# Turning a sample's cached keys on VectorE instead of TensorE, through a DRAM scratch, in a decoder step

## The chip, the cores and the metric

One core of one Trainium2 chip runs the kernel. The metric is the device time of one execution in microseconds (us), as the median of several runs. All arithmetic is float32.

## What is computed

One inference step of a two-layer decoder for a prompt of 256 tokens and a sample group of 8 sequences with one new token each, which share the weights. The first layer mixes by convolution and gating and ends in a dense feed-forward part; the second attends and ends in a mixture of experts. The part that the change touches is the sample's attention over its 1024 cached keys, which lie in pages:

```python
def dsa_attend(q, qi, wi, qpos, kidx, gather_kv, topk):
    dots = jnp.einsum('bthd,bsd->bths', qi, kidx) * (IDX_DIM ** -0.5)
    score = jnp.einsum('bth,bths->bts', wi, jax.nn.relu(dots))
    score = jnp.where(admissible, score, -jnp.inf)
    top_val, sel = lax.top_k(score, topk)
    k_sel, v_sel = gather_kv(sel)
    logits = jnp.einsum('btkgd,btskd->btkgs', qg, k_sel) * (HEAD_DIM ** -0.5)
    p = jax.nn.softmax(jnp.where(valid, logits, -jnp.inf), axis=-1)
    return jnp.einsum('btkgs,btskd->btkgd', p, v_sel)
```

For the prompt the same function runs over its own 256 keys (64 are chosen); for the sample 256 of 1025 are chosen, by page table from cache_k and cache_v. There are 16 query heads, 4 key heads and 64 dimensions a head.

## The kernel before

The five engines run hand-ordered programs that meet in semaphores. The stages, by the semaphore numbers of the finished TensorE groups (eight matmuls of a 128-row output each): input and output projection of the even layer, **up** (G_UP, 44 groups; `hidden` on VectorE multiplies two groups per step m), **down**, the odd layer's input projection (G_OIN, 18 groups, with rotation, index scores and top-k beside it), **attention**, output projection, routing, experts.

In the attention stage the prompt is worked in eight units u = 0 to 7, each one block of 128 queries and four heads; units 0 to 3 see 128 keys, units 4 to 7 see 256. Each unit has two halves. Its steps are: `logits(u)` on TensorE into two PSUM banks; `masked_logits(u)` on VectorE (mask, then row maximum, one of each per half); `exps(u, half)` on ScalarE; `probs_t(u, half)`, transposes on TensorE into bank 6; `probs_by_key(u, half)`, the copy of that bank on ScalarE; `values(u, half)` on TensorE; `heads(u)` on VectorE; `heads_t(u)` on TensorE and `heads_out(u)` on ScalarE. There is one bank 6, so the second half's `probs_t` waits for the copy of the first half. Two buffers S hold the exponentials of neighbouring units.

Between these steps stands the sample's work. The cached keys come from DRAM by indirect DMAs on GpSimd's queue (`gather_k`, 16 of them, 512 KB each), key by row. `k_unit` transposes four 128x128 blocks on TensorE, and `k_copy` on ScalarE moves the result into KT: 32 units of each. `k_logits` multiplies four sequences' keys with the queries, 512 columns each, into banks 2 and 3. The sample's choice of 256 keys is a radix search on VectorE: `radix(s)` counts over 1032 scores, `tally(s)` on TensorE sums the counts, `refine(s)` narrows the threshold; after eight rounds come ties (`eqk`, a scan), the masked logits SS, their maximum, the exponential on ScalarE, transposes, and `sample_values(par)`, 32 matmuls each. `select` finds the prompt's top 64 by rounds of max and match-replace. At the end VectorE writes the sample's heads into yT and raises `so_done`; the output projection on TensorE and the first loads of expert weights on SyncE's queue wait for it.

The input projection's rotation has its cosine part on GpSimd (`cosine`), queued behind `gather_k` of the first four; VectorE's `turn` waits for it.

## Time and profile before

| | us |
|---|---|
| median of 3 runs | 873.46 (873.28 to 873.88) |
| span of the profiled execution, first to last instruction | 871.0 |
| device time around the span, at the median of the runs | 2.5 |
| TensorE busy | 832.9 (96%) |
| VectorE busy | 246.1 (28%) |
| ScalarE busy | 139.4 (16%) |
| GpSimd busy | 98.7 (11%) |
| DMA: moved, mean rate | 206.02 MB, 237 GB/s |

The profiled execution's own device time is not recorded beside its span; 873.46 is taken for it. Busy shares are averages over stages that have different limits. A TensorE line counts matmuls whose ends are modelled, so a busy TensorE need not work at its peak. "PEclk" is the granted TensorE clock as a share of 2.4 GHz: 1.00 is that level and 0.50 is 1.2 GHz. A float32 matmul of the program shows as two records in the trace, a transpose as one.

### The profile page before, as it was taken

What the parts mean: (1) busy time and instruction counts of PE and PEld (TensorE: products, weight loads), DVE (VectorE), ACT (ScalarE), POOL (GpSimd) and SP (SyncE); (2) the same over time, 40 slices, a digit from 0 to 9 for tenths busy, and PEclk for the clock granted to TensorE, in tenths of its full rate; (3) what the DMA queues carried; (4) which work ended last, traced back from release to release, by engine and by line L of the source; (5) the groups of instructions that cost most, each with busy time, mean ns of one, the idle gap of its engine ahead of it and who ended that gap; (6) DMA issues with size and microseconds to landing.
All of it is one profiled execution on the core that took longest, in us unless ns stands there. A gap on an engine that the chain in (4) does not pass through costs nothing.

```text
span 871.0 us, 13710 instructions
## 1 busy us (share of the span) xinstructions
PE 832.9 (96%) x5826; PEld 565.2 (65%) x5826; DVE 246.1 (28%) x706; ACT 139.4 (16%) x342; POOL 98.7 (11%) x146
## 2 busy tenths in 40 slices
PE   6999999999999999999998989999999899999996
PEld 5888878888888888877676566864543343343332
DVE  2173216000000000074566861154422011021025
ACT  0020113000000011131225762121000010000010
POOL 4300300000000000021221410003200001010120
PEclk9999999999999999999997988999999999999998
DMA  9799733448240048897023480977999999999961
GB/s 295 269 376 365 251 97 96 155 136 259 67 133 1 1 136 261 206 218 184 3 96 121 154 334 5 394 278 283 369 410 395 410 392 411 394 394 411 400 254 50
DMA packets 106491, 206.02 MB, mean 237 GB/s; under 512 B 23558, under 2 KB 60818, under 8 KB 105412
## 3 DMA queue, kind: packets, MB, share of 16 engines
q1 hardware_dynamic: 93540, 166.68, 54.5%
q0 software_dynamic: 9264, 31.95, 10.6%
q10 hardware_dynamic: 3632, 6.59, 2.2%
q8 instruction: 43, 0.70, 0.3%
q14 instruction: 12, 0.10, 0.0%
HBM read 192.51 MB, written 12.69 MB: 236 GB/s over the span
## 4 chain that ended last, share of the span: by engine, by line
PE 76%; SPq 9%; DVE 6%; DMA 5%; issue 2%; ACT 2%; DVEq 0%; ACTq 0%
PE ps L685 45%; PE ps L1252 9%; SPq L360 8%; PE ps L1280 3%; DMA scr<-moe_w 2%; DMA slot<-moe_w 2%; PE ps L736 2%; PE ps L1319 2%; PE ps L1072 1%; PE ps L1189 1%; PE ps L1015 1%; PE ps L1088 1%; PE ps L1023 1%; PE ps L898 1%; PE ps L1055 1%
## 5 line engine op out<-in xcount | busy, mean ns | idle before, releaser
L685 PE MATMUL ps<-rw,slot 128*128 128x264 f32 x640 | 142.6, 385 | 0.0
L685 PEld LDWEIGHTS ps<-rw,slot 128*128 128x128 f32 x640 | 120.8, 189 | 21.6
L1252 PE MATMUL ps<-slot,hT 128*32 128x512 f32 x1104 | 123.2, 599 | 3.2 <-DMA slot<-moe_w 3.1
L685 PE MATMUL ps<-xw,slot 128*128 128x264 f32 x512 | 120.6, 392 | 0.8 <-issue 0.8
L685 PEld LDWEIGHTS ps<-xw,slot 128*128 128x128 f32 x512 | 97.0, 192 | 19.4 <-issue 2.3
L1252 PEld LDWEIGHTS ps<-slot,hT 128*32 128x32 f32 x1104 | 40.8, 111 | 80.6 <-issue 69.4
L685 PE MATMUL ps<-hT,slot 128*128 128x264 f32 x352 | 79.8, 386 | 0.0
L685 PEld LDWEIGHTS ps<-hT,slot 128*128 128x128 f32 x352 | 66.3, 190 | 10.9
L1280 PE MATMUL ps<-slot,hT 128*32 128x256 f32 x1216 | 68.1, 380 | 0.0
L685 PE MATMUL ps<-yT,slot 128*128 128x264 f32 x256 | 59.4, 388 | 0.5 <-DVE yT L2082 0.5
L1280 PEld LDWEIGHTS ps<-slot,hT 128*32 128x32 f32 x1216 | 38.2, 110 | 25.7 <-issue 1.0
L685 PEld LDWEIGHTS ps<-yT,slot 128*128 128x128 f32 x256 | 47.8, 190 | 10.2 <-DVE rw L1683 0.8
L1858 DVE TENSOR_TENSOR hT<-silu,ps 128x264 f32<-128x264 f32 x20 | 8.6, 429 | 130.9 <-PE ps L685 130.9
L1623 ACT ACTIVATE silu<-ps 128x256 f32<-128x256 f32 x22 | 8.4, 383 | 210.4 <-PE ps L1252 207.6
L2241 DVE TENSOR_TENSOR yT<-silu,ps 128x256 f32<-128x256 f32 x19 | 8.0, 421 | 110.6 <-ACT silu L1623 110.6
L555 POOL DMA_INDIRECT rw<-cache_k,idx x4 | 3.8, 949 | 293.9 <-PE ps L736 280.1
L1252 PE MATMUL ps<-scr,hT 128*32 128x512 f32 x304 | 34.0, 593 | 0.8 <-DMA scr<-moe_w 0.7
L1434 ACT ACTIVATE silu<-ps 128x264 f32<-128x264 f32 x20 | 7.8, 390 | 128.6 <-PE ps L685 128.6
L1683 DVE SCALAR_TENSOR_TENSOR xw<-rw,ps 128x264 f32<-128x264 f32 x8 | 3.4, 429 | 80.6 <-PE ps L685 80.6
L1252 PEld LDWEIGHTS ps<-scr,hT 128*32 128x32 f32 x304 | 10.1, 110 | 23.3 <-issue 20.2
L639 POOL DMA_DIRECT2D r_rows<-yT x28 | 15.2, 547 | 69.2 <-DVE yT L2246 68.7
L2246 DVE COPY yT<-ps 128x256 f32<-128x256 f32 x19 | 8.1, 425 | 50.3 <-PE ps L1280 50.3
(467 smaller groups left out, 858.3 us busy)
## 6 DMA issues: line engine op xcount, KB each, us to landing
slot<-moe_w SPq DMA_DIRECT2D x50, 1024.0 KB, 19.3
slot<-moe_w SPq DMA_DIRECT2D x16, 2048.0 KB, 15.7
slot<-ffn_w SPq DMA_DIRECT2D x22, 1024.0 KB, 8.0
scr<-moe_w SPq DMA_DIRECT2D x14, 1024.0 KB
slot<-ffn_w SPq DMA_DIRECT2D x8, 1408.0 KB, 6.6
slot<-w_in_even SPq DMA_DIRECT2D x4, 2048.0 KB, 20.5
r_rows<-silu ACTq DMA_DIRECT2D x1, 6144.0 KB, 31.5
slot<-w_out_even SPq DMA_DIRECT2D x2, 2048.0 KB, 24.7
```

Source lines behind the costliest of these rows:

```text
L360: sp.dma_start(dst, src).then_inc(slab_in[s], 16)
L639: pool.dma_start(rows[:, :, 256 * j:256 * j + 256], orow[32 * j:32 * j + 32, 0:nt]).then_inc(rows_stored, 16)
L685: mm = pe.matmul(out, lhs(k), rhs(k), start=(k == 0), stop=(k == n - 1))
L736: mm = pe.matmul(out, lhs(k), scaled[:, k, :], start=(k == 0), stop=(k == KD - 1))
L898: pe.matmul(ps[4][:, 0:T], rot, hT[:, n, :], start=True, stop=True).then_inc(rot_done, 1)
L1015: mm = pe.transpose(ps[i % 2][:, P * r:P * r + P], kraw[n % 2][j][:, 256 * r + P * jj:256 * r + P * jj + P], ident)
L1023: mm = pe.matmul(ps[2 + hf][32 * j:32 * j + 32, :], qw[:, jj, 2 * j + par, 16 - 16 * par:48 - 16 * par], KT[par][:, j, jj, :], start=(par ...
L1055: mm = pe.transpose(ps[6][:, P * (c * nb + k):P * (c * nb + k) + P], S[u % 2][:, half, c, P * k:P * k + P], ident)
L1072: mm = pe.matmul(ps[7][:, P * c + 64 * half:P * c + 64 * half + 64], PT[v % 2][:, P * (c * nb + k):P * (c * nb + k) + P], ktv[:, k, 256 + ...
L1252: mm = pe.matmul(ps[t][32 * j:32 * j + 32, :].rearrange("p (w n) -> p w n", w=2), xgT[:, cap * k + 32 * t:cap * k + 32 * t + 32], moe_slab ...
L1280: mm = pe.matmul(ps[4 + t][32 * j:32 * j + 32, 0:256], hTs[:, t, m % 2, 32 * (m // 2):32 * (m // 2) + 32], moe_slab(4 + m // 4, i)[:, m % ...
L1319: return pe.matmul(ps[4 + half][0:CAP, :], hTl[:, m % 2, m // 2, :], moe_slab(4 + m // 4, i)[:, m % 4, 512 * half:512 * half + 512], start ...
```

## The change

The sample's keys are no longer turned in the attention stage. During the up projection GpSimd gathers each sequence's 1 MB of keys into SBUF (into xw or sqT), VectorE transposes it in 32x32 blocks with one instruction per sequence (`turn_keys`, after every second `hidden` from m = 4 on), and GpSimd stores it with four DMAs into a scratch in DRAM, `k_turned`, in the order the matmuls need. Later eight loads of 1 MB on SyncE's queue bring it back into eight areas. `k_unit`, `k_copy` and the 16 gathers beside the attention are gone; the values are gathered into the same areas once the key products are done. The order of the attention stage on TensorE, ScalarE and VectorE is written anew. The core of the diff:

```diff
...
+        kraw = [flat2(a)[:, 0:2048] for a in (xw, sqT)]
+        kturn = [flat2(yT)[:, 0:2048], cache[:, 0:2048]]
+        area = [[flat2(rw)[:, 0:2048], flat2(sqT)[:, 0:2048], slot[0][:, 0:2048], slot[0][:, 2048:4096]],
+                [slot[2][:, 0:2048], slot[2][:, 2048:4096], slot[3][:, 0:2048], slot[3][:, 2048:4096]]]
...
+            sp.wait_ge(k_turn_stored[1], 256)
...
+            def load_keys(par, j):
+                sp.dma_start(area[par][j], k_turned[2 * j + par]).then_inc(k_in[par], 16)
+            sp.wait_ge(group_done, G_OIN + 4)
+            load_keys(0, 0)
+            load_keys(0, 1)
...
+            sp.wait_ge(sdots_done, 1)
+            load_keys(0, 2)
+            load_keys(0, 3)
+            sp.wait_ge(group_done, G_OIN + 14)
+            load_keys(1, 0)
+            load_keys(1, 1)
+            sp.wait_ge(group_done, G_OIN + 18)
+            load_keys(1, 2)
+            load_keys(1, 3)
...
+            off = lambda b: bass.IndirectOffsetOnAxis(ap=idx[:, b:b + 1].bitcast(U32), axis=0)
+            def gather_k(b):
+                if b >= 2:
+                    pool.wait_ge(k_turn_done, b - 1)
+                pool.indirect_dma_start(out=kraw[b % 2], out_offset=None, in_=krows,
+                                        in_offset=off(b)).then_inc(k_raw_in[b % 2], 16)
+            def store_k(b):
+                pool.wait_ge(k_turn_done, b + 1)
+                for i in range(4):
+                    dst = k_turned[b].rearrange("(u a) (j i x) -> a j u i x", u=4, j=2, i=4)[:, :, :, i]
+                    src = kturn[b % 2][32 * i:32 * i + 32].rearrange("a (j u x) -> a j u x", j=2, u=4)
+                    pool.dma_start(dst, src).then_inc(k_turn_stored[b % 2], 16)
+            def gather_v(par, j):
+                pool.indirect_dma_start(out=area[par][j], out_offset=None, in_=vrows,
+                                        in_offset=off(2 * j + par)).then_inc(v_in[par], 16)
...
-            pool.wait_ge(group_done, G_OIN + 4)
-            for j in range(4):
-                gather_k(0, j)
+                                        in_offset=off(b)).then_inc(ki_in, 16)
+            pool.wait_ge(group_done, G_UP + 4)
+            gather_k(0)
+            gather_k(1)
+            for b in range(TS):
+                store_k(b)
+                if b + 2 < TS:
+                    gather_k(b + 2)
             for q in range(5):
                 cosine(q, q)
             for q in range(5, 7):
                 cosine(q, q + 1)
             for q in range(7, 15):
                 cosine(q, q + 3)
-                if q == 10:
-                    for j in range(4):
-                        gather_k(1, j)
-            for n in range(2, 4):
+            for par in range(2):
+                pool.wait_ge(k_mm, 4 * par + 4)
                 for j in range(4):
-                    pool.wait_ge(k_t, 8 * (n - 2) + 4 + j + 1)
-                    gather_k(n, j)
...
+                    gather_v(par, j)
...
-            def k_unit(n, jj, j):
-                i = 8 * n + 4 * jj + j
-                if jj == 0:
-                    pe.wait_ge(k_in[n % 2][j], 16 * (n // 2 + 1))
-                if i >= 2:
-                    pe.wait_ge(k_copied, i - 1)
-                for r in range(4):
-                    mm = pe.transpose(ps[i % 2][:, P * r:P * r + P],
-                                      kraw[n % 2][j][:, 256 * r + P * jj:256 * r + P * jj + P], ident)
-                mm.then_inc(k_t, 1)
-            def k_logits(n, jj):
-                hf, par = n // 2, n % 2
-                pe.wait_ge(k_copied, 8 * n + 4 * jj + 4)
+            def k_logits(par, hf, jj):
+                if hf == 0 and jj == 0:
+                    pe.wait_ge(k_in[par], 64)
                 for j in range(4):
-                    mm = pe.matmul(ps[2 + hf][32 * j:32 * j + 32, :],
-                                   qw[:, jj, 2 * j + par, 16 - 16 * par:48 - 16 * par], KT[par][:, j, jj, :],
+                    keys = area[par][j].rearrange("p (j i r b) -> p j r i b", j=2, i=4, r=8)[:, jj, 4 * hf:4 * hf + 4]
+                    mm = pe.matmul(ps[2 + hf][32 * j:32 * j + 32, :].rearrange("q (r i b) -> q r i b", r=4, i=4),
+                                   qw[:, jj, 2 * j + par, 16 - 16 * par:48 - 16 * par], keys,
                                    start=(par == 0 and jj == 0), stop=(par == 1 and jj == 1))
                 mm.then_inc(k_mm, 1)
...
             pe.wait_ge(tok_copied, 5)
             logits(0)
-            k_unit(0, 0, 0)
-            k_unit(0, 0, 1)
             pe.wait_ge(key_read, 3)
             pe.wait_ge(qw_done, 1)
             for par in range(2):
@@ -1105,44 +1111,22 @@
                                        qw[:, jj, 2 * j + par, 16 - 16 * par:48 - 16 * par], hT[:, KK + jj, TP:T],
                                        start=(par == 0 and jj == 0), stop=(par == 1 and jj == 1))
             mm.then_inc(own_done, 1)
-            for u in range(4):
-                if u:
-                    k_unit(u, 0, 0)
-                    k_unit(u, 0, 1)
-                    k_logits(u - 1, 1)
-                logits(u + 1)
+            for hf in range(2):
+                for jj in range(2):
+                    k_logits(0, hf, jj)
+            logits(1)
+            for u in range(8):
+                if u < 4:
+                    tally(4 + u)
+                probs_t(u, 0)
+                if 1 <= u < 7:
+                    logits(u + 1)
                 if u:
                     heads_t(u - 1)
-                if u == 0:
-                    tally(4)
-                k_unit(u, 0, 2)
-                k_unit(u, 0, 3)
-                probs_t(u, 0)
-                if u == 0:
-                    tally(5)
-                k_unit(u, 1, 0)
-                if u == 1:
-                    tally(7)
                 probs_t(u, 1)
-                k_unit(u, 1, 1)
-                if u == 2:
-                    pe.wait_ge(key_read, 7)
-                k_logits(u, 0)
-                values(u, 0)
-                k_unit(u, 1, 2)
-                if u == 0:
-                    tally(6)
-                k_unit(u, 1, 3)
-                values(u, 1)
-            k_logits(3, 1)
-            pe.wait_ge(k_copied, 32)
-            logits(5)
-            for u in range(4, 8):
-                probs_t(u, 0)
-                heads_t(u - 1)
-                if u < 6:
-                    logits(u + 2)
-                probs_t(u, 1)
+                if u in (1, 2):
+                    for jj in range(2):
+                        k_logits(1, u - 1, jj)
                 if u == 5:
...
             act.wait_ge(even_stored, 16 * 3)
             act.wait_ge(state_stored, 16)
-            k_copy(0, 0, 0)
-            k_copy(0, 0, 1)
-            exps(0, 0)
-            exps(0, 1)
-            for u in range(4):
+            for u in range(2):
+                exps(u, 0)
+                exps(u, 1)
+            for u in range(8):
+                probs_by_key(u, 0)
                 if u:
-                    k_copy(u, 0, 0)
-                    k_copy(u, 0, 1)
                     heads_out(u - 1)
-                k_copy(u, 0, 2)
-                k_copy(u, 0, 3)
-                probs_by_key(u, 0)
-                k_copy(u, 1, 0)
-                exps(u + 1, 0)
                 probs_by_key(u, 1)
-                k_copy(u, 1, 1)
-                exps(u + 1, 1)
-                k_copy(u, 1, 2)
-                k_copy(u, 1, 3)
-            exps(5, 0)
-            exps(5, 1)
-            for u in range(4, 8):
-                probs_by_key(u, 0)
-                heads_out(u - 1)
-                probs_by_key(u, 1)
-                if u < 6:
-                    exps(u + 2, 0)
-                    exps(u + 2, 1)
                 if u == 4:
...
+                if u < 6:
+                    exps(u + 2, 0)
+                    exps(u + 2, 1)
...
+            def turn_keys(b):
+                dve.wait_ge(k_raw_in[b % 2], 16 * (b // 2 + 1))
+                if b >= 2:
+                    dve.wait_ge(k_turn_stored[b % 2], 64 * (b // 2))
+                V.transpose(kturn[b % 2].rearrange("p (u r a) -> p u r a", u=8, r=8),
+                            kraw[b % 2].rearrange("p (r u a) -> p u r a", r=8, u=8)).then_inc(k_turn_done, 1)
             for m in range(2, 20):
                 silus.k += 1
                 dve.wait_ge(silu_done, silus.base + silus.k)
                 hidden(m, hT[:, m, :])
+                if m >= 4 and m % 2 == 0:
+                    turn_keys(m // 2 - 2)
...
+            masked_logits(1)
+            select(1, range(4, 5))
+            refine(4)
+            radix(5)
+            heads(0)
+            masked_logits(2)
+            refine(5)
+            radix(6)
+            select(1, range(5, 6))
+            heads(1)
+            masked_logits(3)
+            refine(6)
+            radix(7)
+            select(1, range(6, 8))
+            heads(2)
+            masked_logits(4)
+            refine(7)
...
+            heads(3)
...
+            link(V.tensor_tensor_scan(junk, eqk, eqk, 0.0, ALU.add, ALU.bypass))
             masked_logits(5)
...
+            heads(4)
+            masked_logits(6)
...
+            heads(5)
+            masked_logits(7)
+            heads(6)
...
+            heads(7)
```

On TensorE, in unit 1 of the attention (L1055 and now L1063 are `probs_t`, L1041 and now L1049 `logits(2)`, L1081 and L1089 `heads_t(0)`, L1015 `k_unit`, L1023 and L1034 `k_logits`, L908 and L929 `tally`, L1072 and L1080 `values`), before:

```order
L1023 MATMUL ps<-slot,cache 32x512 x4
L1041 MATMUL ps<-hT 128x128 x4
L1081 MATMUL ps<-square,scr 128x128 x2
L1015 MATMUL ps<-square,slot 128x128 x8
L1055 MATMUL ps<-square,scr 128x128 x2
L1015 MATMUL ps<-square,slot 128x128 x4
L908 MATMUL ps<-sst,hT 128x1
L1055 MATMUL ps<-square,scr 128x128 x2
L1015 MATMUL ps<-square,slot 128x128 x4
L1023 MATMUL ps<-slot,cache 32x512 x4
L1072 MATMUL ps<-ktv,scr 128x64 x2
```

and of the change:

```order
L929 MATMUL ps<-sst,hT 128x1
L1063 MATMUL ps<-square,scr 128x128 x2
L1049 MATMUL ps<-hT 128x128 x4
L1089 MATMUL ps<-square,scr 128x128 x2
L1063 MATMUL ps<-square,scr 128x128 x2
L1034 MATMUL ps<-slot,cache 32x512 x8
L1080 MATMUL ps<-ktv,scr 128x64 x4
```

The next unit's logits stood ahead of both `probs_t`; they now stand between the first and the second, and nothing but the heads' transposes stands between them and the second.

On ScalarE in the same unit (L1539 and L1517 are `probs_by_key`, L1529 and L1507 the exponentials, L1521 `k_copy`, L1544 and L1522 `heads_out`), before:

```order
L1544 COPY yT<-ps 128x2x128 [waits ot_done]
L1521 COPY slot<-ps 128x512 [waits k_t] x2
L1539 COPY scr<-ps 128x256 [waits o_done,pt_done]
L1521 COPY slot<-ps 128x512 [waits k_t]
L1529 ACTIVATE scr,fin<-scr,fin 128x128 [waits lg_read]
L1529 ACTIVATE scr,fin<-scr,fin 128x128
L1539 COPY scr<-ps 128x256 [waits o_done,pt_done]
```

and of the change:

```order
L1507 ACTIVATE scr,fin<-scr,fin 128x128 [waits lg_read]
L1507 ACTIVATE scr,fin<-scr,fin 128x128
L1507 ACTIVATE scr,fin<-scr,fin 128x128 [waits lg_read]
L1507 ACTIVATE scr,fin<-scr,fin 128x128
L1517 COPY scr<-ps 128x256 [waits o_done,pt_done]
L1522 COPY yT<-ps 128x2x128 [waits ot_done]
L1517 COPY scr<-ps 128x256 [waits o_done,pt_done]
```

The copy of a unit's first half came ahead of the next unit's exponentials; all four exponentials of the next unit now come ahead of it.

On VectorE, from the masking of unit 5 to that of unit 6 (L1974 and L1978 are mask and maximum, L2027 to L2039 ties and the sample's logits and maximum, L1985 and L1986 `heads(4)`), of the change:

```order
L1974 SCALAR_TENSOR_TENSOR scr<-scr,ps 128x512
L1978 TENSOR_REDUCE fin<-scr 128x2
L2027 SCALAR_TENSOR_TENSOR slot<-slot,sst 128x1032
L2029 TENSOR_TENSOR cache<-cache,slot 128x1024
L2032 TENSOR_TENSOR cache<-cache,slot 128x8
L2035 SCALAR_TENSOR_TENSOR slot<-cache,ps 128x512 x2
L2037 SCALAR_TENSOR_TENSOR slot<-cache,top 128x8
L2039 TENSOR_REDUCE sst<-slot 128x1
L1985 RECIPROCAL fin<-fin 128x4
L1986 TENSOR_TENSOR scr<-ps,fin 128x256
L1974 SCALAR_TENSOR_TENSOR scr<-scr,ps 128x512
```

Before, the ties' two long steps stood ahead of `masked_logits(5)`, and `masked_logits(6)` ahead of `heads(4)`; now the ties and `heads(4)` both stand between `masked_logits(5)` and `masked_logits(6)`.

## Rows read from the trace of the kernel before

**Rows 1.** Windows by stage: length, busy us of each engine, clock, DMA share, GB/s

```profile
140.00:290.00 150.00, 150.00 (x678) 127.34 (x677) 12.33 (x32) 10.65 (x28) 0.00 (x0) 1.00 0.39 123
383.00:459.00 76.00, 72.20 (x362) 53.70 (x360) 42.85 (x126) 17.11 (x43) 18.70 (x23) 1.00 0.43 113
459.00:543.00 84.00, 73.69 (x605) 52.40 (x605) 47.42 (x114) 44.50 (x126) 17.08 (x16) 0.86 0.42 152
543.00:871.00 328.00, 310.74 (x3103) 144.25 (x3103) 81.30 (x262) 33.51 (x81) 37.56 (x61) 0.98 0.90 348
```

**Rows 2.** Windows within the attention stage, columns as in rows 1

```profile
464.00:466.50 2.50, 1.06 (x10) 0.82 (x8) 2.36 (x7) 2.38 (x10) 0.00 (x0) 1.00 0.00 0
473.50:507.50 34.00, 31.39 (x254) 21.07 (x252) 24.61 (x53) 22.32 (x60) 15.03 (x14) 1.00 0.61 212
507.50:511.00 3.50, 0.82 (x9) 0.85 (x9) 3.43 (x7) 2.74 (x11) 0.14 (x1) 1.00 1.01 428
511.00:517.50 6.50, 6.50 (x30) 5.08 (x30) 3.14 (x6) 4.50 (x13) 0.00 (x0) 0.50 1.01 423
```

**Rows 3.** Timeline of TensorE in attention: start, us, what, records, [idle before]

```profile
462.10 1.23 PE L1041 MATMUL ps<-hT 64*128 64x128 f32 x8
469.94 1.94 PE L1023 MATMUL ps<-slot,cache 128*32 128x512 f32 x8
474.53 1.16 PE L1015 MATMUL ps<-square,slot 128*128 128x128 f32 x8
475.62 1.06 PE L1023 MATMUL ps<-slot,cache 128*32 128x512 f32 x8
476.62 0.72 PE L1041 MATMUL ps<-hT 64*128 64x128 f32 x8
510.18 0.63 PE L1055 MATMUL ps<-square,scr 128*128 128x128 f32 x4 [2.68 <-ACT scr L1539]
518.85 1.90 PE L1072 MATMUL ps<-ktv,scr 128*128 128x64 f32 x16
524.18 3.07 PE L1072 MATMUL ps<-ktv,scr 128*128 128x64 f32 x16
535.48 3.66 PE L1088 MATMUL ps<-slot 128*32 128x256 f32 x64
```

**Rows 4.** Timeline of VectorE in attention, columns as in rows 3

```profile
493.63 2.31 DVE L2051 TENSOR_TENSOR_SCAN slot<-slot 128x1032 f32<-128x1032 f32 x1
499.13 0.69 DVE L2007 TENSOR_REDUCE fin<-scr 128x2 f32<-128x512 f32 x1
499.73 1.28 DVE L2053 SCALAR_TENSOR_TENSOR slot<-slot,sst 128x1032 f32<-128x1032 f32 x1
501.05 2.05 DVE L2055 TENSOR_TENSOR cache<-cache,slot 128x1024 f32<-128x1024 f32 x1
...
507.76 0.69 DVE L2007 TENSOR_REDUCE fin<-scr 128x2 f32<-128x512 f32 x1
...
512.92 0.69 DVE L2007 TENSOR_REDUCE fin<-scr 128x2 f32<-128x512 f32 x1
...
520.22 0.69 DVE L2007 TENSOR_REDUCE fin<-scr 128x2 f32<-128x512 f32 x1
...
542.60 0.29 DVE L2082 COPY yT<-ps 128x32 f32<-128x32 f32 x2 [0.23 <-PE ps L1167]
```

**Rows 5.** Timeline of ScalarE in attention

```profile
507.16 0.51 ACT L1529 ACTIVATE scr<-scr,fin 128x256 f32<-128x256 f32 x1 [3.73 <-issue]
509.48 0.56 ACT L1539 COPY scr<-ps 128x512 f32<-128x512 f32 x1
```

**Rows 6.** Timelines of VectorE (up projection), GpSimd and TensorE (input projection)

```profile
154.67 0.43 DVE L1858 TENSOR_TENSOR hT<-silu,ps 128x264 f32<-128x264 f32 x1 [6.69 <-PE ps L685]
388.59 0.76 POOL L570 TENSOR_TENSOR mean<-hT,rope 128x264 f32<-128x264 f32 x1
390.49 0.68 PE L898 MATMUL ps<-hT,square 128*128 128x264 f32 x2 [0.98 <-DVE hT L1886]
```

More of the change, by code:

```diff
@@ L328, in build, with logit_bank @@
         THIN = 64
+        def logit_bank(u, half):
+            return half if u in (5, 7) else 4 + half
         def tiles_at(i):
@@ L2060, in _ @@
-            masked_logits(5)
+            masked_logits(1)
[15 more added lines that the diff above has]
+            refine(7)
+            mark(V.tensor_scalar(eqk[:, 0:1024].rearrange("q (p r) -> q r p", r=8),
+                                 X[:, 0:1024].rearrange("q (r p) -> q r p", r=8), kth, 0.0,
+                                 ALU.is_equal, ALU.add, accum_out=sst[:, 4:5]))
@@ L2061, in _ @@
+            link(V.tensor_tensor(X[:, 1024:1032], X[:, 1024:1032], eqk[:, 1024:1032], ALU.add))
             dve.wait_ge(k_mm, 8)
@@ L2406 @@
     scratch = [nc.dram_tensor(name, shape, F32, kind="Internal").ap()
-               for name, shape in (("r_rows", ((MAXP + 3) * CAP, D)),)]
+               for name, shape in (("r_rows", ((MAXP + 3) * CAP, D)), ("k_turned", (TS, P, 2048)))]
     args += scratch
```

139 lines of the change are left out of this document (40 added, 99 removed).

## Prediction

> **What bounds the kernel now.** I read the windows by stage first. In the up projection TensorE is busy all the time while the DMA engines work at 0.39 of their capacity and VectorE 12.3 of 150 us: there is room for what the change puts there. In the attention stage (459 to 543) the clock is 0.86 and TensorE's 73.7 of 84 us hide idle stretches; from 543 the DMA engines are at 0.90 of capacity over 328 us [rows 1]. That last stage begins for both TensorE and the expert loads with `so_done`, so what the attention stage gains or loses passes to the end one for one. Next, windows inside that stage. From 473.5 to 507.5, units 0 to 3, TensorE is busy 31.4 of 34 us: it is the bound there. Behind it, from 507.5 to 511, it works 0.82 of 3.5 us, while VectorE works 3.43 of them: there the bound is a chain through four engines, and at 510.18 TensorE had waited 2.68 us for a copy on ScalarE [rows 2, 3]. The reader is to see two regimes, since the change takes work from the first and rewrites the order of both.
>
> **The clock.** It was full (2.4 GHz) from 464 to 466.5 while TensorE worked 1.06 of 2.5 us, and soon after, at 469.94, a `k_logits` took twice its usual time. It was full again from 473.5 to 507.5, then came the stretch with 0.82 of 3.5 us of work, and from 511 to 517.5 it was half (1.2 GHz) [rows 2, 3]. So a stretch in which TensorE is mostly idle is followed by half clock, and prices on TensorE come in pairs, full and half: `logits` of a 128-key unit 0.7 and 1.2 us, a `k_logits` 1.0 and 1.9, eight records each; the values of a 256-key unit 1.9 and 3.1 [rows 3]. For 256 keys I double the first, for 128-key values I halve the last (1.0 and 1.5). Transposes of one half are 0.6 us for 256 keys; estimates are 0.9 at half clock, and 0.3 and 0.45 for 128 keys.
>
> **What goes.** 32 units of four transposes: two units take 1.09 us, from 474.53 to 475.62 [rows 3], so 16 x 1.09 = 17 us of TensorE at full clock, and 32 copies of ScalarE. Were TensorE's work the bound of the whole stage, 17 us would be won. It is the bound only in units 0 to 3.
>
> **What comes in the up projection: nothing on the path.** One `turn_keys` moves 2048 elements per partition. Nearest rows: 1.28 us for 1032 and 2.05 us for 1024 elements [rows 4]; so 2.6 to 4.1 us. Between two `hidden` VectorE is idle for 6.69 us [rows 6], so either is covered, and a turn comes only every second step, 14.2 us. The Trainium skill, Vector Engine (DVE) Microarchitecture Reference, section on the reshape front-end, says a 32x32 transpose sustains one element per cycle and lane; by it a turn would take some 2.1 us, which changes nothing. The gathers, stores and later loads carry 8 MB each. Gathers and stores over eight turns, 114 us, are 147 GB/s beside 123 GB/s [rows 1], and the last stage shows 348 GB/s over 328 us, so weight loads stay ahead. If that cover went (a turn later than its `hidden` by more than 6.7 us), each turn would hold the bank release and TensorE. The wait for the stored turns ahead of SyncE's small key-index load is over long before, and the reloads on its queue come behind the weights of the same stage; I cost them at nothing, but a reload that came late would hold the first `k_logits`.
>
> **Input projection: -1.0.** GpSimd's four gathers kept `cosine` until 388.59, and TensorE waited 0.98 us for the rotation behind it [rows 6]. The gathers leave that place.
>
> **Attention, by milestones.** I walk the new order; a hand-over between engines is 0.15 us (a copy from 509.48 to 510.04, its reader at 510.18 [rows 3, 5]). "Masked(u)" is the end of `masked_logits(u)`: 1.35 us per half for 256 keys (0.69 for the maximum, the mask about as long [rows 4]), some 0.8 for 128 by estimate.
>
> (1) Opening. `logits(1)` ran at 462.10 [rows 3]; now four `k_logits` stand ahead: 4.0 to 7.8 us, and the clock is half there, so I take 6.1. Then `logits(1)` 0.7, and from it to `tally(5)` masking, one round of selection, refine and count, 4.4: unit 1 begins at 473.3 (471.2 to 475.5).
>
> (2) Units 1 and 2. Order on TensorE is probs_t, logits(u+1), probs_t of half two; on ScalarE exps(u+1) stand ahead of the copy of half one. So this is a ring with nothing beside it: tally and probs_t 0.5, logits 0.7, masking after it 1.2, last exponential half 0.8, copy 0.4, probs_t 0.3, two `k_logits` 2.0, values 1.0, hand-overs 0.6: 7.5 us at full clock, 10.5 at half. TensorE idles some 3 us in it. I take 9.7 and 9.3. Masked(4) comes 3.8 to 4.4 us into unit 3: 496.4 (490.0 to 500.9). Before it took from 474.53 to 499.8 [rows 3, 4], 25.3 us with all the key work, now 23.1 without it; so little is won although most of the 17 us went here. Against 499.8: **-3.4**.
>
> (3) To masked(5). It stood right behind; now refine, `eqk` 2.5, heads(3), the count below the threshold and the scan (1.3 + 0.4 + 2.3 [rows 4]) and the masking 2.65 stand in a row on VectorE: 10.6 to 11.6, I take 11.3, before 8.7 (to 508.4 [rows 4]): **+2.6**.
>
> (4) To masked(6). Ties 1.3 + 2.05 + 0.2, SS 1.4, its maximum 1.2, heads 0.6, masking 2.65: 9.5 to 10, take 9.8, before 5.2 (508.4 to 513.6 [rows 4]): **+4.6**.
>
> (5) To masked(7). Ring again: exponential half 1.0 [rows 5], copy 0.6, probs_t 0.6, transposes of SS 0.9, values 1.9, probs_t 0.6, logits of one half 0.55, masking 2.65: 8.7 to 12.0, take 10.8, before 7.3 (to 520.9 [rows 4]): **+3.5**.
>
> (6) To `so_done`. Exponential, copy, probs_t, values, sample_values(0) 3.66 + 0.4 [rows 3], then unit 7 with sample_values(1), its values, products and VectorE's write 9.2: 17.7 to 21.4, take 20.3, before 22.0 (to 542.9 [rows 4]): **-1.7**.
>
> Sum: -1.0 - 3.4 + 2.6 + 4.6 + 3.5 - 1.7 = **+4.6 us**. I take the half clock for about six tenths of the distance, since stages (3) to (5) leave TensorE idle for 3 to 6 us a unit, and the case of 507.5 to 511 shows what follows such a stretch. With every TensorE price at full clock the milestones add to -7.4, with every one at half to +12.0. The profiled execution (span 871.0, device time taken as 873.46, the median) becomes span 875.6, device time 878.1, and so the median.
>
> **Rivals.** (A) The clock stays high: 873.5 - 7.4 = **866.1**, faster. Break-even is where under four tenths of the way from full to half is paid (7.4 of 19.4). For it: the full clock lasted 34 us with little but transposes, keys and small products [rows 2, 3]. Against it: in those 34 us TensorE was busy 0.92 of the time, and the ring of (2) leaves it at about 0.6, (3) to (5) under 0.5, near the 0.42 of 464 to 466.5. The Trainium skill, TensorE: Matmul & The Clock Gate, section on transpose mode, says transposes do not count as busy for the clock the way matmuls do. By that rule the removed transposes never held the clock, what held it (`k_logits`, values) is still there, and the time would go towards 866. No row here separates the two kinds: the 34 us at full clock held both. Chance 0.22, most of it faster.
> (B) TensorE's work was the bound and the other engines close up: -17 less what the opening costs, some **859**. Rows 2 show 3.43 of 3.5 us of VectorE when TensorE was free, against it. Chance 0.05.
> (C) Half clock throughout, or hand-overs worse than 0.15: **885.5**. Chance 0.11.
> (D) The turning does not stay hidden: a turn or its gather is over a microsecond later than the idle 6.69 us allow, eight times over: 878 + 8 to 20, **886 to 898**. Against it, the DMA engines are at 0.39 there [rows 1] and a gather has some 14 us. Chance 0.03.
>
> **Numbers.** A measurement of this kernel tells 0.2%, 1.75 us, from no change. Forecast case (slower, 876 to 882) 0.46, C 0.11, D 0.03: slower 0.60. Cases that end within 0.2%, between forecast and A: 0.13. A and B: faster 0.27. The range reaches down towards A, not to its end, and up to C: 868 to 885.5.
>
> **What would show it.** In the changed profile: `turn_keys` under 6.7 us with no TensorE wait in the up projection; TensorE idle ahead of the second `probs_t` of each unit, waiting for ScalarE's copy; unit lengths of 9 to 10 us where 7.5 would mean A; masked(5) to masked(6) near 9.8 us, filled by VectorE; the stage's granted clock below 0.86; the stage behind `so_done` unchanged in length. Wrong if the clock of the stage is near 1, or if `so_done` comes before 542.

## Result and the profile after

The changed kernel takes **881.96 us** (median of 4 runs), the kernel before 873.37 beside it (4 runs); the ratio is 1.0132, 95% interval 1.0096 to 1.0167: slower, though by less than 2%, by 11.5 us at the middle of the interval (0.0132 x 873.4), by 8.6 in the medians. The profiled execution spans 880.4 us (before 871.0), its granted clock is 0.958 (before 0.979).

Windows of the profile after, the up projection, the attention stage (from its first `logits` to the end of the write that releases `so_done`) and what follows it; columns as in [rows 1]:

```profile
140.00:290.00 150.00, 150.00 (x678) 127.32 (x677) 28.52 (x35) 9.43 (x25) 27.06 (x39) 1.00 0.75 235
456.35:551.88 95.53, 68.03 (x477) 44.86 (x477) 47.44 (x114) 27.87 (x93) 7.63 (x8) 0.68 0.28 104
552.00:880.00 328.00, 310.58 (x3103) 140.53 (x3103) 81.41 (x262) 33.53 (x81) 37.57 (x61) 0.98 0.90 348
```

The up projection is full of TensorE's work as before, with 8 MB gathered and 8 MB stored more in it. From `so_done` to the last instruction it is 328.5 us (before 328.1), at 348 GB/s. The loss lies in the attention stage. For the kernel before the same window is

```profile
459.03:542.89 83.86, 73.69 (x605) 52.37 (x605) 47.38 (x114) 44.41 (x125) 17.08 (x16) 0.86 0.42 153
```

so the stage grew by 95.53 - 83.86 = **11.7 us**. The two spans differ by 9.4: behind the stage 0.4 us were lost, and the stage began 2.7 us earlier (456.35 against 459.03). Of these 2.7, 1.7 were there before the change does anything, at the end of the first run of matmuls on loaded weights, 128 records (42.60 us before, 40.94 after):

```profile
11.74 30.86 PE L685 MATMUL ps<-xw,slot 128*128 128x264 f32 x128 [0.83 <-issue]
```

```profile
12.22 28.72 PE L706 MATMUL ps<-xw,slot 128*128 128x264 f32 x128 [0.83 <-issue]
```

(the kernel before first). At the `hidden` that stands at 154.67 in [rows 6] it is still 1.7 us (153.00 after). The other 1.0 us is won in the input projection, as experiment 6 shows. So the change costs -1.0 + 11.7 = **10.7 us**, and 11.1 with the 0.4 behind the stage; the interval of the ratio is 8.4 to 14.6 us.

Over the profiles of the changed program and of the variants below the first `logits` started anywhere from 455.99 to 460.44 us, with the same code ahead of it but for experiment 3. Below I therefore measure each profile by the **length of its attention stage**, first `logits(0)` to `so_done`. It is one profile for each version.

The turns on VectorE, as groups of instructions by line:

```profile
L1827 DVE STREAM_TRANSPOSE yT<-xw 128x2048 f32<-128x2048 f32 x4 | 9.2, 2304 | 0.0
L1827 DVE STREAM_TRANSPOSE cache<-sqT 128x2048 f32<-128x2048 f32 x4 | 9.2, 2304 | 0.0
```

What TensorE waited for in the attention stage (us in total, times, longest):

```profile
PE ps L1063 <- ACT scr L1517: 25.6, 8, 5.7
PE ps L1110 <- DVE key L1930: 1.8, 1, 1.8
```

L1063 is `probs_t`, L1517 ScalarE's copy of the turned probabilities: in every unit the second `probs_t` waits for the copy of the first. ScalarE's timeline in unit 3 shows why that copy is late (columns as in [rows 3]):

```profile
494.07 0.51 ACT L1507 ACTIVATE scr<-scr,fin 128x256 f32<-128x256 f32 x1 [8.42 <-DVE fin L1978]
...
495.39 0.51 ACT L1507 ACTIVATE scr<-scr,fin 128x256 f32<-128x256 f32 x1 [0.22 <-DVE fin L1978]
...
496.39 0.35 ACT L1517 COPY scr<-ps 128x256 f32<-128x256 f32 x1
```

ScalarE stood 8.42 us with nothing to do, in `exps(4)`, before the copy of unit 3 behind it could go. The transposes for that copy had begun at 489.85. The chain of waits, in order of time, is this ring (start, us, what):

```profile
489.99 0.53 PE ps L1063 x2
490.52 2.08 PE ps L1049 x8
...
492.63 0.70 DVE scr L1974
493.35 0.69 DVE fin L1978
494.04 0.61 DVE scr L1974
494.67 0.70 DVE fin L1978
...
495.80 0.68 ACT scr L1507 x3
496.48 0.27 ACT scr L1517
...
496.88 0.66 PE ps L1063 x2
497.54 1.61 PE ps L1080 x8
```

first `probs_t`, `logits(4)`, both halves masked, exponentials, copy, second `probs_t`, values, and nothing beside it. `logits` here took 2.08 us; `logits(7)` of the same profile took 1.14 at full clock.

### The profile page after: what moved, and what is told of

Its sections match the earlier page's. It is cut to its first block, busy times and chain, and to the rows that moved or that the text cites. A ratio compares the mean times of both kernels' runs of the same rounds, so it can differ in the third digit from the quotient of the medians.

```text
span 880.4 us, 13438 instructions
## 1 busy us (share of the span) xinstructions
PE 825.1 (94%) x5698; PEld 552.6 (63%) x5698; DVE 263.9 (30%) x712; ACT 123.0 (14%) x310; POOL 109.7 (12%) x170
## 4 chain that ended last, share of the span: by engine, by line
PE 78%; SPq 8%; DMA 5%; DVE 5%; ACT 2%; issue 1%; ACTq 0%; DVEq 0%
PE ps L706 45%; PE ps L1236 9%; SPq L365 8%; PE ps L757 3%; PE ps L1264 3%; DMA scr<-moe_w 3%; DMA slot<-moe_w 2%; PE ps L1080 2%; PE ps L1303 2%; PE ps L1173 1%; PE ps L1034 1%; PE ps L1096 1%; PE ps L1063 1%; PE ps L1049 1%; DVE fin L1978 1%
## 5 line engine op out<-in xcount | busy, mean ns | idle before, releaser
L706 PE MATMUL ps<-xw,slot 128*128 128x264 f32 x512 | 118.5, 387 | 0.8 <-issue 0.8
L706 PEld LDWEIGHTS ps<-xw,slot 128*128 128x128 f32 x512 | 95.5, 189 | 18.8 <-issue 2.3
L1236 PEld LDWEIGHTS ps<-slot,hT 128*32 128x32 f32 x1104 | 37.2, 111 | 84.6 <-issue 79.5
L1264 PEld LDWEIGHTS ps<-slot,hT 128*32 128x32 f32 x1216 | 38.2, 110 | 26.1 <-issue 1.0
L1063 PE MATMUL ps<-square,scr 128*128 128x128 f32 x48 | 11.6, 368 | 25.6 <-ACT scr L1517 25.6
L1063 PEld LDWEIGHTS ps<-square,scr 128*128 128x128 f32 x48 | 7.7, 201 | 28.3 <-ACT scr L1507 27.2
```

Source lines behind the costliest of these rows:

```text
L706: mm = pe.matmul(out, lhs(k), rhs(k), start=(k == 0), stop=(k == n - 1))
L1063: mm = pe.transpose(ps[6][:, P * (c * nb + k):P * (c * nb + k) + P], S[u % 2][:, half, c, P * k:P * k + P], ident)
L1236: mm = pe.matmul(ps[t][32 * j:32 * j + 32, :].rearrange("p (w n) -> p w n", w=2), xgT[:, cap * k + 32 * t:cap * k + 32 * t + 32], moe_slab ...
L1264: mm = pe.matmul(ps[4 + t][32 * j:32 * j + 32, 0:256], hTs[:, t, m % 2, 32 * (m // 2):32 * (m // 2) + 32], moe_slab(4 + m // 4, i)[:, m % ...
```

## Experiments

All kernels ran beside the kernel before (873 us). "Stage" is the length defined above. In every diff only the moved lines are shown.

**1. ScalarE's order alone.** One index in the loop of ScalarE:

```diff
-            for u in range(2):
-                exps(u, 0)
-                exps(u, 1)
+            exps(0, 0)
+            exps(0, 1)
             for u in range(8):
...
                 probs_by_key(u, 1)
+                if u < 7:
+                    exps(u + 1, 0)
+                    exps(u + 1, 1)
...
-                if u < 6:
-                    exps(u + 2, 0)
-                    exps(u + 2, 1)
```

> The changed kernel with one thing other: ScalarE does exps(u+1) behind probs_by_key(u, 1) instead of exps(u+2), so exps(0) alone stands ahead of the loop. Theory (order): what costs the change its time is that ScalarE's copy of half one of unit u+1 stands behind exps(u+2), whose logits TensorE issues only behind the first probs_t of unit u+1; the 25.6 us that TensorE waited in L1063 for L1517 are this ring. With it cut they fall below 8 us, the attention stage's clock rises from 0.68 to over 0.8, masked_logits to masked_logits takes 7 to 9 us where it took 9 to 11.8, and the time is 855 to 867 us, below the kernel before (873.4). Rival (clock first): TensorE stays at half clock whatever ScalarE does, its own work then takes 8 to 9 us in a unit, and the time is 873 to 879. Rival (keys or VectorE): the loss lies in the trips of the keys or in VectorE's ties, and the time stays at 880 to 883.

Measured: 864.48 us, ratio 0.9902 (0.9876 to 0.9928), so faster than the kernel before. Stage and waits of TensorE:

```profile
460.44:535.46 75.02, 59.69 (x477) 38.77 (x477) 47.05 (x114) 28.25 (x93) 7.63 (x8) 0.77 0.36 133
```

```profile
PE ps L1089 <- DVE scr L1985: 4.8, 2, 3.6
PE ps L929 <- DVE sst L1916: 3.7, 3, 2.1
PE ps L1063 <- ACT scr L1507: 3.1, 1, 3.1
...
PE ps L1063 <- ACT scr L1517: 1.7, 3, 0.6
```

The 25.6 us of waiting for the copy became 1.7, the stage 20.5 us shorter. Clock 0.77 is under the 0.8 I expected; the time is as expected. The change's loss is this order of ScalarE's: with the ring cut the stage is 8.8 us below that of the kernel before. How much of these 8.8 us comes from the turned keys and how much from the rest of the new order is not shown, since no run gives the new order to the kernel that turns on TensorE.

**2. Unread work in TensorE's waits, matmuls or transposes.** The changed kernel, ahead of the second `probs_t` of units 0 to 5; the output stays unused:

```diff
+                if u in (4, 5):
+                    pe.wait_ge(lg_read, 2 * u + 2)
+                if u < 6:
+                    fill(ps[5 if u == 4 else 1], 4)
                 probs_t(u, 1)
```

> The changed kernel with four matmuls of 512 columns more (identity by a constant, into a free bank, never read) ahead of the second probs_t in each of units 0 to 5, where TensorE waited 2.4 to 5.7 us for ScalarE: 24 x 592 ns = 14.2 us at full clock. Nothing else is changed. Theory (the idle costs twice, once as a wait and once as clock): the clock of the attention stage rises from 0.68 to over 0.85, values and probs_t of a unit take near half of what they took, and the time falls by 5 to 15 us to 867 to 877 although TensorE does more. Rival (the ring alone): the clock does not matter since the chain runs through VectorE and ScalarE, and the time is 880 to 886. Rival (the work is simply in the way): 886 to 896.

> The same as e2_fill_matmul with nine 128x128 transposes in place of the four matmuls (9 x 272 ns = 2.4 us at full clock, as long as these). If transposes keep the clock as matmuls do, stage clock and time are those of e2_fill_matmul within 2 us. If a transpose does not count as work for the clock, the clock stays at 0.6 to 0.72 and the time is 880 to 892, over e2_fill_matmul by 5 us or more.

Measured: 875.84 us with matmuls, ratio 1.0036 (1.0017 to 1.0054), and 875.50 with transposes, ratio 1.0045 (1.0024 to 1.0066). The stages, matmuls first, transposes below:

```profile
459.66:548.13 88.47, 76.70 (x525) 46.73 (x525) 47.47 (x114) 27.86 (x93) 7.63 (x8) 0.87 0.31 113
```

```profile
455.99:544.25 88.26, 66.21 (x531) 46.92 (x531) 47.38 (x114) 27.86 (x93) 7.63 (x8) 0.83 0.31 113
```

More work on TensorE made the stage 7.1 and 7.3 us shorter: at least so much of the 11.7 us is the half clock that the waits bring. The other 4.6 and 4.4 us remain at a stage clock (0.87 and 0.83) near the 0.86 of the kernel before; it is not at full clock throughout, so they are not the ring alone. Both kinds of filler give the same time, though they are not as long as each other as I had priced them: four matmuls took 3.60 us at full clock, nine transposes 1.15.

```profile
475.21 3.60 PE L1103 MATMUL ps<-square 128*128 128x512 f32 x8
```

```profile
478.20 1.15 PE L1103 MATMUL ps<-square 128*128 128x128 f32 x9
```

The clock shows most plainly in units 1 and 2 and at the start of unit 3; from 470 to 490 us the changed kernel, then the one with transposes:

```profile
470.00:490.00 20.00, 14.86 (x85) 7.89 (x85) 11.39 (x37) 5.12 (x22) 1.65 (x2) 0.67 0.41 163
```

```profile
470.00:490.00 20.00, 13.80 (x117) 9.00 (x116) 15.04 (x41) 7.47 (x32) 3.74 (x4) 1.00 0.59 227
```

TensorE is busy for 0.69 of the stretch against 0.74 (at half clock the same work counts longer), and the clock is 1.00 where it was 0.67, with 1.15 us of transposes in each wait. The Trainium skill, TensorE: Matmul & The Clock Gate, section on PE-mode transpose, says of a 128x128 transpose that it does not count as busy in the same way. These windows and the two equal times do not bear that out for 128x128 transposes in float32. From 490 to 510 us the two fillers part: the clock is 0.91 with matmuls and 0.66 with transposes, against 0.59 in the changed kernel. No run has fillers of equal length, so what of this is the kind of work and what its length is open.

**3. Each turn done twice.**

> The changed kernel with each of the eight 32x32-block turns of the keys done twice in a row on VectorE: 8 x 2.3 = 18.4 us of VectorE's time more in the up projection. Theory: the turning is wholly hidden there, TensorE waits for nothing in L's of the up projection, and the time stays within 1 us of the changed kernel (881 to 883). Rival: a part of the 8.6 us comes from the turning or the trips that it holds up, and the time grows by 3 to 18 us.

Measured: 883.77 us, ratio 1.0123 (1.0095 to 1.0151). VectorE's 28.5 us of that window are now 49.6 (18.4 of the 21.1 more are the second turns, the rest is work that the later start moves into it), TensorE's 150.00 of 150 remain, and the stage of attention is the changed kernel's to 0.1 us:

```profile
140.00:290.00 150.00, 150.00 (x678) 127.33 (x677) 49.60 (x50) 11.56 (x29) 27.99 (x40) 1.00 0.74 235
458.92:554.35 95.43, 67.93 (x477) 44.78 (x477) 47.45 (x114) 27.85 (x93) 7.64 (x8) 0.68 0.28 105
```

The turning is free, and two turns in a row still fit. The median is 0.8 us over the range I gave, in executions from 881.2 to 885.8. No stage in the trace grew: its first `logits` came 2.6 us later than in the changed kernel, and so did the `hidden` ahead of the first turn (162.70 against 160.12 us).

**4. The opening, on the version of experiment 1 and on the changed kernel alone.** TensorE's order only:

```diff
             pe.wait_ge(qw_done, 1)
+            k_logits(0, 0, 0)
             pe.wait_ge(key_read, 3)
...
-            for hf in range(2):
-                for jj in range(2):
-                    k_logits(0, hf, jj)
             logits(1)
+            k_logits(0, 0, 1)
...
                 probs_t(u, 0)
+                if u == 0:
+                    k_logits(0, 1, 0)
...
                 probs_t(u, 1)
+                if u == 0:
+                    k_logits(0, 1, 1)
```

> e1_act_order (864.5 us) with the opening in another order on TensorE: one of the four k_logits of unit pair 0 goes where it waited 1.8 us for key_read ahead of the own products, logits(1) comes right behind these, and the other three k_logits fill the waits of unit 0 (behind logits(1), behind each probs_t). In e1_act_order VectorE stood 5.5 us idle before masked_logits(1) and was busy without a break from 477 to 511 us, so it is the bound there. Theory: masked_logits(1) comes 3 to 5 us earlier, smax_done and so_done 2 to 4 us, and the time is 860.5 to 862.5. Rival: TensorE owes the same products and is behind by as much in units 0 to 2, VectorE's wait moves to heads(0) and masked_logits(2), and the time stays at 864 to 865.

> The changed kernel (882.0 us) with the opening of e4_opening alone and ScalarE's order as changed. Theory: masked_logits(1) comes 3 to 5 us earlier, but the ring of copy, second probs_t, values, first probs_t, logits and exps sets units 1 to 4 whatever VectorE has in hand, and the k_logits that move into unit 0 lie in the ring's wait; so the gain of the opening is kept: 877.5 to 880.5. Rival: the k_logits come back in the ring, the time stays within 1 us (881 to 883).

Measured: 858.00 us on experiment 1, ratio 0.9825 (0.9802 to 0.9848), stage 68.7; and 879.75 alone, ratio 1.0073 (1.0046 to 1.0099), stage 89.3.

```profile
459.14:527.83 68.69, 56.15 (x477) 37.26 (x477) 46.89 (x114) 28.22 (x93) 7.63 (x8) 0.83 0.39 145
```

Both gain 6.3 us of stage, the first more than expected (860.5 to 862.5 us). The four products had taken 4.9 us in the changed kernel (459.80 to 464.70), between two steps that VectorE waits for. The rest of the gain goes with a higher clock (0.77 to 0.83 on experiment 1); that the clock is its cause is argued and not shown. That alone, too, the gain is kept whole shows that the ring of the later units does not absorb it: it starts earlier by as much.

**5. `logits(u+1)` ahead of the first `probs_t`, ScalarE's order as changed.**

```diff
-                probs_t(u, 0)
                 if 1 <= u < 7:
                     logits(u + 1)
+                probs_t(u, 0)
```

> The changed kernel (882.0 us) with TensorE's logits(u+1) ahead of the first probs_t of unit u and not behind it, all else as changed, ScalarE's order too. It cuts the same ring at another place: exps(u+1), which stand ahead of the first copy of unit u on ScalarE, then have their logits one transposing step (0.4 to 1.1 us) earlier, but still ahead of that copy. Theory: the ring gets shorter by that step in six units and by the clock that this gives back, but is not cut: 873 to 880, far from the 864.5 of e1_act_order. Rival (only TensorE's order counts): 862 to 868. Rival (the ring is elsewhere): 881 to 883.

Measured: 880.94 us, ratio 1.0113 (1.0085 to 1.0140), stage 93.3, that is 2.2 us shorter than the changed kernel's. TensorE still waits, and for the same copy:

```profile
PE ps L1063 <- ACT scr L1517: 23.1, 8, 5.7
```

The ring only lost a step. The time lies above the 873 to 880 that I expected, and its interval does not part it from the changed kernel's. In unit 4 the `exps` wait for VectorE's count and scan, whatever TensorE issues first. So it is the place of `exps(u+2)` on ScalarE that matters, and this order on TensorE does not make up for it.

**6. The kernel before with its four raw gathers behind the first cosines.**

```diff
-            pool.wait_ge(group_done, G_OIN + 4)
-            for j in range(4):
-                gather_k(0, j)
             for q in range(5):
                 cosine(q, q)
+            pool.wait_ge(group_done, G_OIN + 4)
+            for j in range(4):
+                gather_k(0, j)
```

> The kernel before (873.4 us) with one edit: GpSimd issues the four gathers of raw keys gather_k(0, j) behind its five first cosines and not ahead of them. It tells what of the gain in the input projection (attention's first logits at 456.35 us, 459.03 before) comes from these four issues alone. Theory: all 2.7 us, since the cosine is kept 2.7 us by them (388.59 against 385.93) and the projection's later waits follow it: time 870.3 to 871.5. Rival: only the 1.0 us that TensorE waited in L919's place comes back, the rest is VectorE's or ScalarE's: 872 to 873. Rival: nothing, since the gathers collide with loads later: 873.4 or more.

Measured: 870.33 us, ratio 0.9971 (0.9955 to 0.9986), that is 2.5 us less (1.2 to 3.9). By the number alone my theory holds; by the trace the input projection gives 1.0 us of it and not 2.7. The `hidden` that stands at 154.67 in [rows 6] and the first cosine, this run first, the changed kernel below:

```profile
156.02 0.43 DVE L1858 TENSOR_TENSOR hT<-silu,ps 128x264 f32<-128x264 f32 x1 [6.69 <-PE ps L685]
388.94 0.75 POOL L570 TENSOR_TENSOR mean<-hT,rope 128x264 f32<-128x264 f32 x1 [283.79 <-ACT hT L1454]
```

```profile
153.00 0.43 DVE L1817 TENSOR_TENSOR hT<-silu,ps 128x264 f32<-128x264 f32 x1 [6.69 <-PE ps L706]
385.93 0.74 POOL L602 TENSOR_TENSOR mean<-hT,rope 128x264 f32<-128x264 f32 x1 [120.75 <-ACT hT L1438]
```

Between the two it is 232.9 us in both, and 388.59 - 154.67 = 233.9 in the kernel before. From the cosine to the first `logits` (459.38, 456.35 and 459.03) it is 70.4 us in all three. So the four gathers held the cosine, and with it the start of attention, by 1.0 us. TensorE's wait for the rotation shows the same, from 383 to 462 us in the kernel before and then here:

```profile
PE ps L898 <- DVE hT L1886: 1.3, 2, 1.0
```

```profile
PE ps L898 <- DVE hT L1886: 0.3, 1, 0.3
```

A further 1.3 us lies in the attention stage, 82.6 us against 83.9; what of that is the edit and what is chance is not shown.

**7. VectorE's ties, and the sample's chain.** Experiment 4 with `masked_logits(5)` ahead of the running count, `heads(4)` and `masked_logits(6)` ahead of the sample's own logits; then the same with ScalarE's and TensorE's part of the sample behind unit 5 and `heads(5)` and `masked_logits(7)` ahead of VectorE's reciprocal (the diff shows VectorE in the first):

```diff
+            masked_logits(5)
             link(V.tensor_tensor_scan(junk, eqk, eqk, 0.0, ALU.add, ALU.bypass))
-            masked_logits(5)
...
+            heads(4)
...
+            masked_logits(6)
...
-            heads(4)
-            masked_logits(6)
```

> e4_opening with VectorE's ties in another order: masked_logits(5) ahead of the running count (2.3 us), heads(4) ahead of the two additions to X, masked_logits(6) ahead of the sample's own logits. In e1_act_order TensorE waited 3.1 us for exps(5) and 3.6 us for heads(4) and fell to half clock from 495 to 512 us. Theory: both waits shrink to under 2 us in all, TensorE is at half clock for less of that stretch, units 5 and 6 end 3 to 5 us earlier, while smax_done comes 3 us later; since TensorE's work is the end's bound, the time is 1 to 4 us below e4_opening. Rival: the sample's chain (smax_done, exp, transposes, sample_values) is the bound, and the time rises by 1 to 3 us.

> e5_ties (861.3 us) with the sample's softmax behind unit 5 on the other engines: ScalarE does exps(6) ahead of the sample's exp, TensorE the eight transposes of SS behind values(5), VectorE the reciprocal behind masked_logits(7). In e5_ties TensorE waited 8.4 us for the copy of unit 5, which stood behind the sample's exp on ScalarE. Theory: that wait goes, units 5 and 6 run while VectorE does the ties, the time is 3 to 6 us below e5_ties and 0 to 3 below e4_opening: 855 to 858. Rival: the sample's chain is the end's bound and the 8.4 us were in its shadow: 860 to 862.

Measured: 861.25 us, ratio 0.9860 (0.9834 to 0.9886), stage 74.0, for the first, against 0.9825 and 68.7 of experiment 4: my theory failed. The reason was the same fault again, a step that waits ahead of a step that could go. The sample's exponential now waited longer on ScalarE, and the copy of unit 5 stood behind it:

```profile
PE ps L1063 <- ACT scr L1520: 9.0, 2, 8.4
```

With that moved, 856.05 us, ratio 0.9820 (0.9796 to 0.9844), stage 68.5: the wait is gone, another stands in its place

```profile
PE ps L1144 <- ACT slot L1542: 5.6, 1, 5.6
```

(the transposes of the sample's probabilities), and the stage is that of experiment 4 (68.7). Working on the prompt's units first or on the sample first comes to the same here: the maximum of the sample's logits is ready 40.8 us into the stage in experiment 4 and 45.0 here, and from there to `so_done` it takes 27.9 and 23.5 us.

**8. Filler where TensorE waits for the ties.** Experiment 4 with ten unread matmuls, two ahead of `heads_t(2)`, four behind `values(4)`, four ahead of `heads_t(4)`:

> e4_opening (858.0 us) with unread matmuls of 512 columns on TensorE where it stood idle for VectorE's ties: two ahead of heads_t(2), four behind values(4), four ahead of heads_t(4); 10 x 592 ns = 5.9 us at full clock. In e4_opening TensorE went at half clock from 485 to 515 us, with 14 us of own work from 501 to 516. Theory (there the clock and not a wait sets the end): the clock of 480 to 520 rises from about 0.68 to over 0.85, the sample's first values end 3 to 5 us earlier, and the time is 852.5 to 856. Rival: the filler does not raise the clock, or is itself in the way, and the time is 858 to 862.

Measured: 856.97 us, ratio 0.9824 (0.9800 to 0.9849).

```profile
458.52:526.88 68.36, 60.38 (x497) 37.52 (x497) 46.85 (x114) 27.95 (x93) 7.63 (x8) 0.95 0.39 146
```

The clock of the stage went from 0.83 to 0.95, its length from 68.7 to 68.4: next to nothing, and the time lies above the 852.5 to 856 that I expected. From 480 to 500 us, where the clock rose from 0.63 to 1.00, VectorE was busy 19.38 of 20 us in both, experiment 4 first:

```profile
480.00:500.00 20.00, 12.38 (x62) 9.13 (x58) 19.38 (x33) 6.66 (x22) 1.88 (x2) 0.63 0.53 211
```

```profile
480.00:500.00 20.00, 16.64 (x79) 9.53 (x78) 19.38 (x34) 7.03 (x22) 1.49 (x2) 1.00 0.49 206
```

The chain went through VectorE there: the maximum of the sample's logits is ready 40.8 us into the stage in both. From 500 to 527 us, where TensorE is busy 24 of 27 us, the clock had been 0.83 and is 0.87, so little could be won there. A risen clock went with 7 us in the ring of experiment 2 and with 0.3 us beside a busy VectorE.

**9. Combined.** Experiment 8's idea on the second version of 7, the sample's exponential ahead of `exps(6)` again, `masked_logits(6)` behind the maximum of the sample's logits, three unread matmuls behind `values(5)`:

> e8_sample_later (856.1 us) with the sample's chain ahead again where it waits for nothing of the prompt: VectorE does masked_logits(6) behind smax_done, ScalarE the sample's exp ahead of exps(6), and three unread matmuls of 512 columns (1.8 us at full clock) stand on TensorE behind values(5), where it waited 5.6 us for the sample's exp. Theory: smax_done comes the 2.8 us earlier that masked_logits(6) takes, TensorE's wait shrinks to 1 to 3 us, so_done comes 1.5 to 3 us earlier, and the time is 853 to 854.6. Rival: unit 6 is held up by as much behind its later logits, and the time is 856 to 858.

Measured: 854.06 us (851.1 to 857.5), ratio 0.9795 (0.9760 to 0.9830). The median lies where I expected it by luck, since the mechanism did not work: the stage is 68.5 us as in 7 and 8. The sample's exponential was done at 501.2, but the transposes that read it began at 505.05, since the three matmuls ahead of them took this long:

```profile
499.92 5.30 PE L1103 MATMUL ps<-square 128*128 128x512 f32 x6
505.05 1.04 PE L1150 MATMUL ps<-square,slot 128*128 128x128 f32 x8
```

I had priced them at 1.8 us; three would be 2.7 by the full-clock row of experiment 2 (4 in 3.60), and here they ran at half. This version and those of 4, 8 and the second of 7 can't be told apart by their stages. All four are faster than both kernels, with ratios of 0.9795 to 0.9825 to the one before.

## Why the direction was right and the size was not

The input projection is measured from the `hidden` of experiment 6 to the first `logits`; the other lengths are counted from the first `logits`, before [rows 3, 4] against after. "Masked(u)" is the end of `masked_logits(u)`, as in the prediction.

| step of the prediction | forecast | measured |
|---|---|---|
| up projection | 0 | 0 |
| input projection | -1.0 | 303.4 - 304.4 = -1.0 |
| (1), (2) to masked(4) | -3.4 | 39.0 - 40.8 = -1.8 |
| (3) to masked(5) | +2.6 | 11.2 - 8.6 = +2.6 |
| (4) to masked(6) | +4.6 | 11.8 - 5.2 = +6.7 |
| (5) to masked(7) | +3.5 | 11.1 - 7.3 = +3.8 |
| (6) to `so_done` | -1.7 | 22.4 - 22.0 = +0.4 |
| sum | +4.6 | +10.7 |

**Right.** The ring of step (2), its order and its place, was read from the code as it ran: TensorE idle ahead of the second `probs_t`, unit 1 at 13.8 us into the stage (forecast 14.3), units 1 and 2 of 10.4 and 9.0 us (9.7 and 9.3). Step (3) came out to a tenth. The turns took 2.30 us each, below my range of 2.6 to 4.1; the room of 6.69 us [rows 6] covered them, and in experiment 3 twice as much. The rate in the Trainium skill, Vector Engine (DVE) Microarchitecture Reference, section on the reshape front-end, one element per cycle and lane, had given an estimate of 2.1 us, which is near. The last stage passed the loss on one for one (328.5 us against 328.1). The input projection won the forecast 1.0 us, and the gathers were what it had waited for (experiment 6).

**Wrong in size: the half clock.** "I take the half clock for about six tenths of the distance" is the sentence that failed. The measured 10.7 us lie at 0.93 of the distance from -7.4 to +12.0. From 490 us to `so_done` most terms that TensorE sets came at their price at half clock; from 524.99 to 527.04 and behind 541 they did not. In step (4) I had VectorE as the bound with 9.8 us; it waited 2.29 us more for `logits(6)`, as its timeline shows:

```profile
512.96 0.42 DVE L1986 TENSOR_TENSOR scr<-ps,fin 128x256 f32<-128x256 f32 x1
515.67 0.69 DVE L1974 SCALAR_TENSOR_TENSOR scr<-scr,ps 128x512 f32<-128x512 f32 x1 [2.29 <-PE ps L1049]
```

and TensorE ahead of that went through values, transposes and logits with no wait at all, each at its price at half clock:

```profile
508.31 1.09 PE L1063 MATMUL ps<-square,scr 128*128 128x128 f32 x4 [5.69 <-ACT scr L1517]
509.19 3.51 PE L1080 MATMUL ps<-ktv,scr 128*128 128x64 f32 x16
512.50 1.06 PE L1063 MATMUL ps<-square,scr 128*128 128x128 f32 x4
513.49 2.09 PE L1049 MATMUL ps<-hT 64*128 64x256 f32 x8
```

The 5.69 us of idling in the first of these rows is what came ahead, as with the 0.82 of 3.5 us before [rows 2]. At full clock the four steps take 0.6, 1.9, 0.6 and 1.1 us, which would have put `logits(6)` ahead of VectorE. The same holds for `logits(4)` in unit 3 (2.08 us), a part of the 1.6 us missed in (2), and for (6): values(6) took 3.51 us, to 535.8, and the products of `sample_values(0)` went on to 541.87, 6.1 us for 3.66 at full clock. The sum with every price at half clock came to +12.0, and +10.7 was measured. The change came out nearer to the case that I called C, and gave 0.11, than to my forecast, though the clock of the stage was 0.68 and not 0.5 throughout. That the two medians lie only 8.6 us apart, nearer to the forecast 4.6, is in part luck: when an execution's attention begins moves by more than 1.7 us by itself. I had also taken 0.2% as what a measurement can tell; the interval of the ratio is 0.35% to each side.

**Rival A** (clock stays high, 866.1) had both its parts wrong. The clock fell; and when filler raised it to 0.87 (experiment 2) the stage was still 4.6 us longer than before, where A's sum has it 6.4 shorter. A clock near 1 all through this order was in no run. Its ground, that transposes do not count, is contradicted by the same experiment from 470 to 490 us. **Rival B** (859, TensorE's work as the bound) fell with the 25.6 us that TensorE waited. Experiment 4 comes to 858.0, but by another order and with VectorE as the bound from 480 to 500 us. **Rival D** fell with experiment 3. What the prediction did not ask is how little would undo the ring; the forecast is for an order, and one index on ScalarE was worth 20.5 us of stage.

## What to carry to other kernels

When work goes from a busy engine, look first at what each in-order queue will stand at: a step that waits for something late must not stand ahead of one whose input is ready, since everything behind the one that waits stops with it. Where a ring through several engines leaves TensorE waiting in every unit, as it did here for 25.6 of 95.5 us, price its steps at half clock too, and compare a change by the lengths of its stages, each from a step that both programs have, and not by the span. Filler paid here where TensorE's own steps lay on the chain (7 us); beside a VectorE that was busy throughout it gained 0.3 us, and three matmuls of it ran at half clock themselves and were in the way (5.30 us).

## What was not expected of the hardware

- A turn of 128 partitions by 2048 float32 values in 32x32 blocks takes 2304 ns, 1.12 ns for an element of a partition; the scan over half as many elements takes the same 2.31 us.
- Unread work in the waits shortened the kernel. From 470 to 490 us the clock was 1.00 with 1.15 us of 128x128 transposes in each wait, as with 3.60 us of 512-column matmuls; from 490 to 510 us it was 0.66 and 0.91.
- With the same code ahead, attention began anywhere from 455.99 to 460.44 us, and executions of the kernel before took 868.3 to 875.3 us. Between the two kernels compared here 1.7 us of it were there by the end of the first 128 matmul records on loaded weights, which took 30.86 us in one and 28.72 in the other. Why is open.
- The clock at the first `logits` is not fixed by the code ahead of it: they took 0.72 us in some executions (experiments 1 and 4) and 1.23 or 1.24 in others (the changed kernel, experiment 3 and the matmul filler), with the same instructions in front.
